# Runs of 512-column products on TensorE in lengths of nine, six or seven instead of eight

## The reference, cut to what matters

```python
s1 = jnp.einsum('thc,hkc->thk', q[:, :, 0], sub_keys1)
s2 = jnp.einsum('thc,hkc->thk', q[:, :, 1], sub_keys2)
v1, i1 = lax.top_k(s1, PEER_TOPK)          # PEER_TOPK is 16
v2, i2 = lax.top_k(s2, PEER_TOPK)
cand = (v1[..., :, None] + v2[..., None, :]).reshape(T, PEER_HEADS, PEER_TOPK * PEER_TOPK)
vc, ic = lax.top_k(cand, PEER_TOPK)
...
pre = jnp.einsum('td,tkd->tk', xb, u)      # u: the up vectors of the chosen experts
a = jax.nn.gelu(pre) * gb
return jnp.einsum('tk,tkd->td', a, expert_v[ib])
```

## Time and profile before

| what | value |
|---|---|
| median of 3 runs | 1536.97 us (1535.47 to 1537.46) |
| profiled execution | 1535.1 us |
| its span, first to last instruction | 1533.3 us |
| TensorE busy | 98% of the span |
| VectorE, ScalarE, GpSimd busy | 83%, 57%, 15% |
| first mlp, wide strips | from 119 us to 292 us of the span |
| second mlp, wide strips | from 426 us to 600 us |
| peer, first half of the up strips | from 788 us to 957 us |
| peer, second half of the up strips | from 957 us to 1163 us |

### The profile page before, as it was taken

How to read it: one execution, slowest core, us unless ns; L and a number is a source line. 1 busy time by engine, 2 the same in 40 slices (tenths; PEclk the granted TensorE clock), 3 DMA queues, 4 the chain that set the end, 5 groups by cost and what they waited for, 6 DMA issues and landing times.

```text
span 1533.3 us, 29887 instructions
## 1 busy us (share of the span) xinstructions
PE 1509.4 (98%) x10088; PEld 1302.7 (85%) x10088; DVE 1273.8 (83%) x2434; ACT 880.0 (57%) x1408; POOL 230.3 (15%) x99
## 2 busy tenths in 40 slices
PE   8899999999999999999999999999999999999999
PEld 7788888889888888998998888888888888878887
DVE  8978888845788888786789986899999999998887
ACT  7964444568753445765666666555554444455553
POOL 1010000125100001000778747200000000000000
PEclk9999999999999999999999999999999999999999
DMA  6145655553566555444456566555555555565563
GB/s 233 44 155 177 191 190 181 176 165 111 155 207 193 188 189 178 151 127 167 151 162 192 178 185 199 179 176 168 175 171 167 170 176 173 170 232 183 188 214 116
DMA packets 72501, 264.67 MB, mean 173 GB/s; under 512 B 8048, under 2 KB 8304, under 8 KB 72048
## 3 DMA queue, kind: packets, MB, share of 16 engines
q1 hardware_dynamic: 69696, 253.63, 51.6%
q10 hardware_dynamic: 2736, 10.11, 1.7%
HBM read 262.66 MB, written 1.05 MB: 172 GB/s over the span
## 4 chain that ended last, share of the span: by engine, by line
PE 81%; DVE 13%; ACT 3%; issue 2%; DMA 1%; DVEq 0%; ACTq 0%; SPq 0%
PE ps L796 31%; PE ps L652 21%; PE ps L656 11%; DVE arena L2038 4%; PE ps L620 2%; PE ps L1307 2%; PE ps L624 2%; PE ps L621 2%; PE ps L710 1%; DVE w_lo L2038 1%; PE ps L1376 1%; PE ps L1377 1%; PE ps L1378 1%; DVE arena L2712 1%; DVE arena L2713 1%
## 5 line engine op out<-in xcount | busy, mean ns | idle before, releaser
L1426 ACT ACTIVATE w_hi<-ring 128x1024 fp32r<-128x1024 f32 x475 | 500.1, 1057 | 330.9 <-PE ps L796 181.4
L2038 DVE TENSOR_TENSOR w_lo<-ring,w_hi 128x1024 fp32r<-128x1024 f32 x383 | 465.8, 1218 | 55.8 <-ACT w_hi L1426 50.0
L652 PE MATMUL ps<-tokens_r,w_hi 128*128 128x512 f32 x1696 | 427.9, 394 | 2.2 <-DVE arena L2038 1.1
L652 PEld LDWEIGHTS ps<-tokens_r,w_hi 128*128 128x128 f32 x1696 | 306.0, 188 | 60.4 <-DVE arena L2038 1.8
L3049 POOL TENSOR_TENSOR w_lo<-ring,w_hi 128x1024 fp32r<-128x1024 f32 x92 | 225.2, 2458 | 737.9 <-DVE w_lo L2038 391.4
L796 PE MATMUL ps<-w_hi,halves_hi 128*128 128x512 f32 x632 | 250.4, 396 | 1.3 <-DVE halves_lo L2038 1.1
L796 PE MATMUL ps<-w_hi,halves_lo 128*128 128x512 f32 x632 | 247.0, 391 | 0.0
L656 PEld LDWEIGHTS ps<-tokens_r,w_lo 128*128 128x128 f32 x1696 | 227.7, 188 | 18.1 <-DVE w_lo L2038 0.7
L656 PE MATMUL ps<-tokens_r,w_lo 128*128 128x256 f32 x1696 | 232.4, 279 | 0.0
L796 PE MATMUL ps<-w_lo,halves_hi 128*128 128x512 f32 x632 | 170.5, 390 | 0.0
L2038 DVE TENSOR_TENSOR arena<-arena 128x256 f32<-128x256 f32 (+6 forms) x273 | 145.6, 547 | 8.6 <-ACT arena L1634 2.1
(11 more groups left out here) (378 smaller groups left out, 1980.2 us busy)
## 6 DMA issues: line engine op xcount, KB each, us to landing
ring<-in_strips SPq DMA_DIRECT2D x475, 512.0 KB, 3.4
arena<-in_pairs ACTq DMA_DIRECT2D x14, 512.0 KB, 4.9
const<-in_const SPq DMA_DIRECT2D x1, 1384.0 KB, 11.0
x_s<-in_x SPq DMA_DIRECT2D x2, 512.0 KB, 4.4
arena<-in_rel ACTq DMA_DIRECT2D x1, 1024.0 KB, 4.8
arena<-in_keys ACTq DMA_DIRECT2D x1, 1024.0 KB, 5.8
out<-x_s SPq DMA_DIRECT2D x4, 256.0 KB, 2.1
arena<-in_ssm_bc SPq DMA_DIRECT2D x1, 512.0 KB, 7.5
```

Of the source, the lines that this page charges most:

```text
L652: pe.matmul(bank, w[0][:, c * P:(c + 1) * P], hT[:, c].rearrange("p s t -> p (s t)"), start=c == 0, stop=False, skip_group_check=True)
L1426: sc.activation(w_hi[:, n % RING, :], ring[:, n % RING, :], ACT.Copy).then_inc(high_ready, 1)
L2038: return ve.tensor_tensor(o, a, b, op)
```

## The change

`strip_wide` is split into `wide_high` (some of the 512-column products) and `wide_low` (the wait for the low half and the 256-column products). With `late=k` the last k wide products come behind the low ones. `three_wide` does three strips a, b, c in the order: eight of a, one of b, lows of a; seven of b, two of c, lows of b; six of c, lows of c. The runs of wide products are then 9, 9 and 6 long.

- `gate_up` does the gate strip with `late=1` and the up strip as before: 7 wide, lows, 1 + 8 wide, lows.
- The first half of peer goes by `three_up` in triples; the last four strips, behind the loop, stay. The waits of a strip (`high_ready`, `up_sum`, and `key_out` once) stand ahead of its first product, and so ahead of the lows of the strip before.
- The second half of peer, in its loop of 60 strips, does odd strips with `late=2`: 8 wide, lows, 6 wide, lows, 2 wide, scatters.

The products, their operands and their number, the strips' order, the ring and all other engines' programs are unchanged.

```diff
-            def strip_wide(bank, w, fresh=None):
-
-                for c in range(KC):
+            def wide_high(bank, w, chunks, fresh=None):
+
+                for c in chunks:
                     input_ready(fresh, c)
-                    pe.matmul(bank, w[0][:, c * P:(c + 1) * P], hT[:, c].rearrange("p s t -> p (s t)"),
-                              start=c == 0, stop=False, skip_group_check=True)
+                    mm = pe.matmul(bank, w[0][:, c * P:(c + 1) * P], hT[:, c].rearrange("p s t -> p (s t)"),
+                                   start=c == 0, stop=False, skip_group_check=True)
+                return mm
+
+            def wide_low(bank, w):
+
                 low_halves(w)
                 for c in range(KC):
                     mm = pe.matmul(bank[:, 0:T], w[1][:, c * P:(c + 1) * P], hT_hi[:, c, :], start=False,
                                    stop=c == KC - 1, skip_group_check=True)
+                return mm
+
+            def strip_wide(bank, w, fresh=None, late=0):
+
+                wide_high(bank, w, range(KC - late), fresh)
+                mm = wide_low(bank, w)
+                if late:
+                    mm = wide_high(bank, w, range(KC - late, KC))
                 mm.then_inc(strip_done, 1)
+
+            def three_wide(banks, ws, fresh=None):
+
+                for n, early in enumerate((0, 1, 2)):
+                    wide_high(banks[n], ws[n](), range(early, KC), fresh if n == 0 else None)
+                    if n < 2:
+                        wide_high(banks[n + 1], ws[n + 1](), range(0, early + 1))
+                    wide_low(banks[n], ws[n]()).then_inc(strip_done, 1)
...
-                    for part in range(2):
-                        strip_wide(ps[:, bank + 2 * part, :], split(strip + part, i))
+                    strip_wide(ps[:, bank, :], split(strip, i), late=1)
+                    strip_wide(ps[:, bank + 2, :], split(strip + 1, i))
...
-                def up(e, i=None):
+                def up_weights(e, i=None):
...
-                    strip_wide(ps[:, up_bank(e), :], w, 6 if e == 0 and i is None else None)
+                    return w
+
+                def up(e, i=None, late=0):
+
+                    strip_wide(ps[:, up_bank(e), :], up_weights(e, i), late=late)
+
+                def three_up(first, i=None):
+
+                    held = {}
+
+                    def weights(e):
+                        if e not in held:
+                            held[e] = up_weights(e, i)
+                        return held[e]
+
+                    es = [first + n for n in range(3)]
+                    three_wide([ps[:, up_bank(e), :] for e in es], [lambda e=e: weights(e) for e in es],
+                               6 if first == 0 and i is None else None)
...
-                for e in range(UNROLL):
-                    up(e)
+                for e in range(0, UNROLL, 3):
+                    three_up(e)
                 with pe.Fori(1, HALF // UNROLL) as i:
-                    for e in range(UNROLL):
-                        up(e, i)
+                    for e in range(0, UNROLL, 3):
+                        three_up(e, i)
...
-                        up(HALF + u, i)
+                        up(HALF + u, i, late=2 * (u % 2))
                         pair_behind(0, u, i)
```

## The result

| | before | changed |
|---|---|---|
| median of 16 runs | 1535.82 us | 1544.66 us |
| lowest, highest | 1534.87, 1542.74 us | 1538.06, 1551.97 us |
| profiled execution, its span | 1535.1, 1533.3 us | 1539.37, 1537.6 us |

The ratio of the changed kernel to the kernel before is 1.0042, with a 95% interval of 1.0027 to 1.0056, so +4 to +9 us. A second measurement of it (12 runs) gave 1.0017, 0.9996 to 1.0037. Seven of the 16 runs lie between 1538.06 and 1539.70 us, and the profiled one is among them.

A forecast was written before the change was run, and what follows sets the result against it. TensorE, busy 98% of the span, was taken as the bound, with VectorE nearly full in peer's first half. Mlps -3.2, second half 0 and first half +13.1 gave +9.9 us on 1536.97, so 1546.9; range 1532.0 to 1550.0.

The forecast's parts named there:

- rival (1): First half of peer: VectorE's second operation still goes first, only shorter stalls grow; +1.2 us in all, 1538.2; chance 0.18.
- The mlps: Gate and up strips: both low groups become short, -0.08 us per chunk, 40 chunks, -3.2 us (-3.4 to -1.0).
- Second half: Second half of peer: a pair of strips takes 6.09 us against 6.10, so 0 (-1.2 to +1.4 us).
- The race: First half of peer: GpSimd's low half leads VectorE's second two-input SBUF operation by 0.09 us and holds it, 2.19 us later.
- The lag at the first operation: First half of peer: VectorE's first two-input operation starts about 0.2 us behind GpSimd, so it is held 2.07 us.
- One stall: First half of peer, strip 14: TensorE stalls 0.45 + 2.19 = 2.64 us for VectorE's sum.
- How often it comes: First half of peer: four second operations held (strips 14, 20, 26, 32), 2.7 us, then three cycles of 3.0 us.
- rival (2): First half of peer: VectorE's first operation escapes too, waits vanish by strip 14; -3.5 us in all, 1533.4; chance 0.25.
- term of 11.7 us: First half of peer: the long stalls at strips 14, 20, 26 and 32 together cost 11.7 us.
- strips 0 to 13: Start of the first half of peer: +0.6 us taken, between -0.2 and +0.9, VectorE's early routing operations being held too.
- Strips 33 to 59: Later first half of peer: earlier waits at third strips, such as strip 35, cost +0.8 us (-0.5 to +2.0).
- Rival (3): Whole kernel: low group length doesn't depend on the run ahead, no group gets shorter; 1537 us; chance 0.07.

The follow-up runs named there:

- e10: Against the kernel before, only the mlps changed, with two late products instead of one (6 wide, lows, 2 + 8 wide, lows): 1537.09 us, ratio 1.0005.
- e3: Against the kernel before, only the second half of peer gets the new order, odd strips with two late products: 1536.57 us, ratio 1.0007.
- e11: The whole changed kernel measured once more against the kernel before, with a second trace: 1539.03 us, ratio 1.0017.
- e2: Against the kernel before, only the first half of peer gets the triples: 1541.70 us, ratio 1.0035.
- e5: The whole change, with GpSimd waiting for VectorE's sums ahead of low halves 6k and 6k + 1, against the kernel before: 1533.93 us, ratio 0.9971.
- e9: Against the kernel before: mlps' new order, triples for strips 0 to 29 only, GpSimd yields as in e5, old second half: 1530.32 us, ratio 0.9946.
- e8: Against the kernel before: triples in first half of peer alone, GpSimd yields only at VectorE's second operation (strips 6k + 2): 1542.12 us, ratio 1.0046.
- e1: Against the kernel before, only the mlps get the new order, peer as before: 1532.32 us, ratio 0.9986.
- e7: Against the kernel before: mlps' new order, peer's products in old order, GpSimd yields as in e5: 1531.83 us, ratio 0.9971.

## Why the prediction came out as it did

It forecast 1546.9 us, slower, by +9.9 us. Measured are slower and +6.4 us by ratio (+4 to +9), and +4.3 in the profiled execution; by the medians of the second measurement it is +2.8 (1539.03 against 1536.22). That the first median, 1544.66, lies so near the forecast is in part luck. Both traces of the changed kernel have one long stall and not four, and seven of the 16 runs lie at 1538.06 to 1539.70 us, beside the 1538.2 that rival (1) gave by another mechanism.

- **The mlps: right.** -3.2 was forecast, -3.16 measured (stages), chunks of 8.24 us as worked out. e10 shows that the rule behind it, and not the split, does it.
- **Second half: right in kind.** 0 forecast within -1.2 to +1.4; a pair takes 6.10 us where 6.09 was summed, +0.35 in all (6.12 and +0.9 in e3 and e11).
- **The race: right.** A lead of 0.09 us of GpSimd at the second operation was forecast; it is 0.08 in the changed kernel and 0.07 and 0.10 in e2 (831.59 - 831.52, 851.24 - 851.14), and VectorE is held each time. The lag at the first operation, put at 0.2, is 0.11 in e2 (845.78 - 845.67). The Trainium skill's page "SBUF — State Buffer", section "SBUF: two separate sides", says that the one that starts first keeps the other out for the whole instruction; the traces agree down to 0.07 us, and e5 shows that the stalls end when VectorE always starts first.
- **One stall: right.** 2.64 us were forecast; the distance of the two products is 2.91 us in the trace (read to the ns), less a usual 0.23: 2.68. Strip 8, put at 0.6 with the strips around it, waits 0.57.
- **How often it comes: wrong for the common course.** The step "There are four second operations (strips 14, 20, 26, 32)", with three cycles of 3.0 us behind the first, failed. The cycle itself was right: 19.54 forecast, 19.65 and 19.66 in e2. But it was taken for granted that the places of the engines repeat. In the changed kernel's trace the granted clock falls behind the first stall; the two low groups and the run between them take 1.71 + 2.18 + 0.95 us instead of 0.91 + 1.37 + 0.91, 1.65 us more, which I had no term for. That sets TensorE back, and GpSimd by as much: from the held second operation to GpSimd's low half beside the next first operation it is 836.76 - 821.05 = 15.71 us, against 845.67 - 831.59 = 14.08 in e2, 1.63 more. VectorE's next first operation comes only 0.93 later than in e2 (15.12 against 14.19), so it leads by 0.59 us where in e2 it lags by 0.11. From there the course of the forecast's rival (2) runs: no operation held up to 875 us. So the term of 11.7 us measured 2.7 + 1.65 and some 0.3 of a small wait, 4.6, and the first half came to +6.4 instead of +13.1. Read from the starts of low groups, against the kernel before, it is +0.47 up to strip 11 (+0.6 was taken for strips 0 to 13), +4.45 from there to strip 32 and +1.46 behind, together +6.38. In e2's trace the fall came behind the third stall, and there the first half is +13.1; three stalls and a slow clock there make up what the forecast had as four stalls.
- **Strips 33 to 59: right in sign.** +0.8 was taken within -0.5 to +2.0, and +1.5 came. The wait ahead of strip 35 grew from 0.27 us to 1.21 us in the changed kernel and 1.26 in e5, because it is the third of its triple; e9, with the old order there, has 0.27 again. A wait of 0.88 us that the kernel before has ahead of strip 33 is gone in the changed kernel; the prediction does not name it.
- **Rival (1)** put its first half at +4.4; e8, which makes it true, has +5.4; a part of the difference is that the first operation is held 2.2 us instead of 2.07 in each cycle.
- **Rival (3)** falls: eight equal products take 0.91 or 0.94 us by where the run ahead of them ended (e1, e10). The Trainium skill's page "TensorE: Matmul & The Clock Gate", section "Wait — 56ns, not 53.3ns?", has a fixed cost per product, and these rows differ from it.

What stays open: why the granted clock fell behind the first long wait in the changed kernel's two traces and only behind the third in e2's. The waits were alike (2.52 us in the two; 2.52, 2.50 and 2.49 in e2).

## What to carry to other kernels

A change that speeds up one engine by a quarter of a microsecond can lose ten times that where two other engines contend, so look up which start leads by how little before moving the engine that paces them. Where VectorE and GpSimd meet at every turn of a loop, let the one off the path wait by a semaphore rather than leave it to their starts: e5, e7 and e9 gained from a wait that was added. And when stalls are summed over a loop, ask whether one of them changes the places for the next turn.

## What was not expected of the hardware

- A wait of TensorE of 2.5 us can cost 1.65 us more behind it, by a granted clock of 0.66 in the 4 us from 826 us on, and not each such wait does.
- Eight 256-column products take 0.91 or 0.94 us by the run ahead of them, and runs of 9, 9 and 6 in peer or of 7 and 9 in the mlps hold it at the lower value turn after turn (strips 2 to 29 in e9; e1), while 6 and 10 in the mlps hold it at the higher (e10).
